# First norm's modulation columns: products on TensorE in four column groups in place of a chain on VectorE

## The reference

```python
mod = jax.nn.silu(c) @ w_ada[l] + b_ada[l]              # (1, 1024) @ (1024, 6144)
sh1, sc1, g1, sh2, sc2, g2 = jnp.split(mod, 6, axis=-1)
h = rms_norm(x, g_mix_norm[l]) * (1.0 + sc1[:, None]) + sh1[:, None]
proj = h @ w_in[l]                                      # q_lat (512 columns), kv_lat (256), ...
```

## Time and profile before

| | |
|---|---|
| device time, median of 3 runs | 1748.63 us (1746.57 to 1749.33) |
| span of the profiled execution | 1746.4 us |
| TensorE busy | 1692.4 us, 97% of the span |
| VectorE busy | 1093.3 us, 63% |
| ScalarE busy | 744.9 us, 43% |
| GpSimd busy | 298.0 us, 17% |
| mean granted TensorE clock | 0.992 |
| chain that ended last | TensorE 84%, VectorE 6%, ACT 4%, SP's queue 2% |

### The profile page before, as it was taken

The page is one execution under the profiler, slowest core; times in us unless marked ns, Lnnn a source line. Parts: engine busy times, 40 slices in busy tenths (PEclk is TensorE's granted clock), DMA queues, the critical chain, the costliest instruction groups (busy, mean ns, idle before and its releaser), DMA issues.

```text
span 1746.4 us, 32411 instructions
## 1 busy us (share of the span) xinstructions
PE 1692.4 (97%) x12781; PEld 1504.0 (86%) x12781; DVE 1093.3 (63%) x1748; ACT 744.9 (43%) x1111; POOL 298.0 (17%) x286
## 2 busy tenths in 40 slices
PE   5999999999999999899999999999999999999998
PEld 4776666788888888799999999999999999989986
DVE  6766576777764668855858664344753766754633
ACT  4467575454332342532323545346323643322323
POOL 2112196210000002432005221110102000000002
PEclk8999999999999999999999999999999999999999
DMA  9453532443333232264335752332543233332332
GB/s 310 124 141 102 157 110 84 135 97 107 99 95 98 84 108 67 85 172 124 127 105 152 224 141 87 99 117 80 166 117 96 74 94 91 92 97 85 96 95 75
DMA packets 321167, 201.18 MB, mean 115 GB/s; under 512 B 51279, under 2 KB 303814, under 8 KB 320918
## 3 DMA queue, kind: packets, MB, share of 16 engines
q1 hardware_dynamic: 300976, 160.79, 32.4%
q0 software_dynamic: 7952, 24.83, 4.7%
q10 hardware_dynamic: 12118, 13.88, 2.3%
HBM read 177.75 MB, written 17.24 MB: 112 GB/s over the span
## 4 chain that ended last, share of the span: by engine, by line
PE 84%; DVE 6%; ACT 4%; SPq 2%; issue 2%; DMA 1%; POOL 1%; ACTq 0%; DVEq 0%; POOLq 0%
PE ps L1467 69%; SPq L854 2%; PE ps L1608 1%; DVE wlo L2175 1%; PE ps L1769 1%; PE ps L1667 1%; PE ps L1779 1%; PE ps L1795 1%; PE ps L2020 1%; PE ps L1682 1%; PE ps L1584 1%; ACT whi L912 1%; DMA xrow<-in_x_dram 1%; PE ps L1946 0%; PE ps L1536 0%
## 5 line engine op out<-in xcount | busy, mean ns | idle before, releaser
L1467 PE MATMUL ps<-zhi,whi 128*128 128x258 f32 (+2 forms) x2072 | 639.2, 308 | 1.4 <-ACT ub L1201 0.6
L1467 PE MATMUL ps<-zlo,whi 128*128 128x258 f32 (+2 forms) x2072 | 633.4, 306 | 0.0
L1467 PE MATMUL ps<-zhi,wlo 128*128 128x258 f32 (+2 forms) x2072 | 632.1, 305 | 0.0
L1467 PEld LDWEIGHTS ps<-zhi,whi 128*128 128x128 f32 x2072 | 390.8, 189 | 25.5 <-issue 2.2
L2175 DVE TENSOR_TENSOR wlo<-stage,whi 128x1024 fp32r<-128x1024 f32 x256 | 324.9, 1270 | 136.0 <-ACT whi L912 124.0
L1467 PEld LDWEIGHTS ps<-zlo,whi 128*128 128x128 f32 x2072 | 390.2, 188 | 19.7 <-issue 1.2
L1467 PEld LDWEIGHTS ps<-zhi,wlo 128*128 128x128 f32 x2072 | 390.9, 189 | 18.0
L912 ACT ACTIVATE whi<-stage 128x1024 fp32r<-128x1024 f32 x256 | 269.4, 1055 | 305.2 <-PE ps L1467 253.7
L1467 PE MATMUL ps<-ghi,whi 128*128 128x512 f32 x340 | 134.7, 396 | 0.0
L1467 PE MATMUL ps<-glo,whi 128*128 128x512 f32 x340 | 134.2, 395 | 0.0
L1467 PE MATMUL ps<-ghi,wlo 128*128 128x512 f32 x340 | 134.0, 394 | 0.0
(11 more groups left out here) (432 smaller groups left out, 2833.5 us busy)
## 6 DMA issues: line engine op xcount, KB each, us to landing
stage<-in_w_up_dram SPq DMA_DIRECT2D x88, 512.0 KB, 3.8
stage<-in_w_in_dram SPq DMA_DIRECT2D x74, 512.0 KB, 4.0
stage<-in_w_down_dram SPq DMA_DIRECT2D x32, 512.0 KB, 4.0
ring<-in_w_ada_dram POOLq DMA_DIRECT2D x24, 512.0 KB, 4.4
adab<-in_w_ada_dram SPq DMA_DIRECT2D x16, 512.0 KB, 7.8
stage<-in_w_down_dram SPq DMA_DIRECT2D x16, 384.0 KB, 3.4
stage<-in_w_o_dram SPq DMA_DIRECT2D x8, 512.0 KB, 4.1
ring<-in_w_ada_dram SPq DMA_DIRECT2D x8, 512.0 KB, 3.7
```

The lines of the kernel that those rows point to most:

```text
L1467: last = pe.matmul(out, w(a, k), x(k, t0, t1), start=(k == 0 and a is whi and x is x_hi), stop=(k == ks - 1 and a is wlo))
```

## The change

The multiplication by silu(c) moves from VectorE to TensorE. `block_rows(r)` multiplies the blocks of round r, as moving columns, with weights `csil32` that hold column k of silu(c) 32 times. Four row tiles k go to the four groups of 32 PSUM partitions of bank 7 (m = 0 to 3), in two halves that add up: eight fp32 matmuls of 128x512 on 128*32 tiles. VectorE copies the bank to `acol`, and `block_sums` adds over the partitions with a column that is one on every 32nd partition.

Bank 7 is then no longer free for `scaled_turn`, which goes between banks 5 and 6 and waits for the zhi of the tile two before it. The transposes of most parameters and of the meta tokens (`setup_turns`) move behind turn 3, with their copies; only b_ada and g_mix are transposed first. SP's order is changed: two units of w_in go ahead of two w_ada blocks each. The order of TensorE's and VectorE's work is written anew.

```diff
+    misc[:, 2] = p % 32 == 0
...
-        XN_AT = (2, 3, 6, 7, 8, 9, 10, 11)
+        XN_AT = (3, 4, 5, 6, 9, 10, 11, 12)
+        MODULATED = (3, 6, 7, 8)
+        ROWS_MM, SUMS_MM = [2 * r + 1 for r in range(4)], [2 * r + 2 for r in range(4)]
+        NFIRST = ROW["g_ql"]
...
-            return ps[:, 5 + k % 3, :]
+            return ps[:, 5 + k % 2, :]
...
-            for u in range(4, 10):
+            for u in range(4, 8):
                 ada_block(u)
             load_unit(sp, 2, unit_views("ql", 2))
-            for u in range(10, 14):
+            for u in range(8, 12):
                 ada_block(u)
             load_unit(sp, 3, unit_views("ql", 3))
-            for u in range(14, 16):
+            for u in range(12, 16):
                 ada_block(u)
...
             act.activation(csil[:, :], ps[:, 2, 0:KD], ACT.Silu).then_inc(act_setup, 1)
+            act.activation(csil32[:, :, :], ps[:, 2, 0:KD].unsqueeze(2).to_broadcast([P, KD, 32]), ACT.Silu).then_inc(act_setup, 1)
...
             def scaled_turn(k):
 
-                if k == 2:
-                    pe.wait_ge(dve_setup, 3)
-                elif k > 2:
-                    pe.wait_ge(zhi_done, k - 2)
+                if k >= 2:
+                    pe.wait_ge(zhi_done, k - 1)
...
+            def block_rows(r):
+
+                if r:
+                    pe.wait_ge(acol_done, r)
+                else:
+                    pe.wait_ge(act_setup, 2)
+                for half in range(2):
+                    u = 4 * r + 2 * half
+                    for v in (u, u + 1):
+                        pe.wait_ge(bulk_in[v % 8], 16 * (v // 8 + 1))
+                    for m in range(4):
+                        mm = pe.matmul(ps[32 * m:32 * m + 32, 7, :].rearrange("p (a b) -> p a b", a=2),
+                                       csil32[:, 4 * half + m, :], adab[:, u:u + 2, m, :], start=half == 0, stop=half == 1)
+                mm.then_inc(mod_mm, 1)
...
+            block_rows(0)
+            pe.wait_ge(dve_setup, 1)
+            pe.wait_ge(xt_done, KD)
+            scaled_turn(0)
+            scaled_turn(1)
             block_sums(0)
             scaled_turn(2)
             first_products(0, (0, 1))
             first_products(1, (0, 1))
+            block_rows(1)
             scaled_turn(3)
+            setup_turns()
             block_sums(1)
-            scaled_turn(4)
+            pe.wait_ge(dve_setup, 5)
             first_products(0, (2,))
             first_products(1, (2,))
+            first_products(2, (0, 1, 2))
+            scaled_turn(4)
+            block_rows(2)
+            first_products(3, (0, 1, 2))
+            block_sums(2)
             scaled_turn(5)
-            block_sums(2)
-            first_products(2, (0, 1, 2))
-            first_products(3, (0, 1, 2))
-            scaled_turn(6)
-            scaled_turn(7)
             for k in range(4):
                 first_products(k, (3,))
+            first_products(4, range(4))
+            scaled_turn(6)
+            block_rows(3)
+            first_products(5, range(4))
             block_sums(3)
-            for k in range(4, KD):
-                first_products(k, (0, 1, 2))
-            for k in range(4, KD):
-                first_products(k, (3,))
+            scaled_turn(7)
+            first_products(6, range(4))
+            first_products(7, range(4))
...
+            def columns(r):
+
+                dve.wait_ge(mod_mm, ROWS_MM[r])
+                dve.tensor_copy(acol[r % 2][:, :, :], ps[:, 7, :].rearrange("p (a b) -> p a b", a=2)).then_inc(acol_done, 1)
...
+            columns(0)
+            split_lo(0)
+            modulation(0)
             split_lo(1)
-            modulation(0)
-            columns(1, 0, 2)
             z_low_first(0)
             z_low_first(1)
-            columns(1, 2, KD)
-            for r in (1, 2):
-                columns(r + 1, 0, 2)
-                modulation(r)
-                split_lo(r + 1)
-                columns(r + 1, 2, KD)
-                z_low_first(2 * r)
-                z_low_first(2 * r + 1)
+            columns(1)
+            setup_copies()
+            modulation(1)
+            split_lo(2)
+            z_low_first(2)
+            z_low_first(3)
+            columns(2)
+            modulation(2)
+            split_lo(3)
+            z_low_first(4)
+            z_low_first(5)
+            columns(3)
             modulation(3)
```

More of the change, by code:

```diff
@@ L621, in piece @@
             return t[0], len(t), 0 if GROUPS[g]["w"] == 64 else 2
-        n_par = sum(1 + ((ROW[n] + k - 1) // P - ROW[n] // P) for n, _, k in PARAMS) + 0
+        n_par = sum(1 + ((ROW[n] + k - 1) // P - ROW[n] // P) for n, _, k in PARAMS) - 2
         n_par2 = sum(r for _, _, r in HEAD_PARAMS)
@@ L1496, in scaled_turn, with setup_turns @@
             def scaled_turn(k):
-                if k == 2:
-                    pe.wait_ge(dve_setup, 3)
-                elif k > 2:
-                    pe.wait_ge(zhi_done, k - 2)
+                if k >= 2:
+                    pe.wait_ge(zhi_done, k - 1)
                 for t in range(QB):
-                    mm = pe.matmul(ps[:, 5 + k % 3, t * P:(t + 1) * P], xrow[:, t, k * P:(k + 1) * P], diag[:, t, :],
+                    mm = pe.matmul(ps[:, 5 + k % 2, t * P:(t + 1) * P], xrow[:, t, k * P:(k + 1) * P], diag[:, t, :],
                                    start=True, stop=True)
                 mm.then_inc(start_mm, 1)
[L1507 to L1521, removed]
+            def setup_turns():
+                pe.wait_ge(dve_setup, 2)
+                pe.wait_ge(s_par, 16 * n_par)
+                pe.wait_ge(s_par2, 16 * n_par2)
+                for b in range(NBLK):
+                    r = min(P, NROWS - b * P)
+                    mm = pe.transpose(ps[:, 1, b * P:b * P + r], prow[0:r, b, :], const("ident", r, r))
+                mm.then_inc(start_mm, 1)
+                pe.wait_ge(s_meta, 16)
+                for k in range(KD):
+                    mm = pe.transpose(ps[:, 3, k * META:(k + 1) * META], metar[:, k * P:(k + 1) * P],
+                                      const("ident", META, META))
+                mm.then_inc(start_mm, 1)
             def last_job(n, x_hi, x_lo, ks, between=None, behind=None):
@@ L2236, in table @@
                 dve.tensor_scalar(a, a, PI, -PI, ALU.min, ALU.max).then_inc(tab_ready, 1)
-            def column(r, k):
-                u = 4 * r + 2 * (k // 4)
-                o, w, c = acol[r % 2][:, :, :], adab[:, u:u + 2, k % 4, :], csil[:, k:k + 1]
-                if k % 4 == 0:
-                    for v in (u, u + 1):
-                        dve.wait_ge(bulk_in[v % 8], 16 * (v // 8 + 1))
-                if k == 0:
-                    if r >= 2:
-                        dve.wait_ge(mod_mm, r - 1)
-                    link(dve.tensor_scalar(o, w, c, None, ALU.mult))
-                elif k < KD - 1:
-                    link(dve.scalar_tensor_tensor(out=o, in0=w, scalar=c, in1=o, op0=ALU.mult, op1=ALU.add))
-                else:
-                    dve.scalar_tensor_tensor(out=o, in0=w, scalar=c, in1=o, op0=ALU.mult, op1=ALU.add).then_inc(acol_done, 1)
-            def columns(r, k0, k1):
-                for k in range(k0, k1):
-                    column(r, k)
+            def columns(r):
+                dve.wait_ge(mod_mm, ROWS_MM[r])
+                dve.tensor_copy(acol[r % 2][:, :, :], ps[:, 7, :].rearrange("p (a b) -> p a b", a=2)).then_inc(acol_done, 1)
             def modulation(r):
-                dve.wait_ge(mod_mm, r + 1)
+                dve.wait_ge(mod_mm, SUMS_MM[r])
                 for i in range(2):
```

39 lines of the change are left out of this document (21 added, 18 removed).

## The result

The changed kernel takes 1763.13 us (median of 6 runs, 1760.4 to 1765.85); the kernel before, timed beside it, 1748.01. The ratio is 1.0085, with a 95% interval from 1.0073 to 1.0096: it is slower, by 15.1 us, where 7.9 were forecast and 1762 was the top of the range. The profiled execution has a span of 1760.8 us, 14.4 more than before.

What follows compares the result with a forecast made beforehand. TensorE was taken to bound the kernel. Start -1.4, rows +5.55, setup turns +1.28, new waits +6.8, old waits -3.3, clock -1.0 make +7.9: span 1754.3, median 1756.5 us (2.2 above the span), range 1747 to 1762.

Steps and rivals of the forecast that it cites:

- What bounds the kernel, and the sign: Whole kernel: TensorE bounds it, VectorE's relief counts only where TensorE waited; slower 0.72, within 0.16, faster 0.12.
- The first product: Start of the first norm's products: 30.3 us instead of 31.66, a gain of 1.4.
- block_rows: Row blocks on TensorE: 1.85 us each, blocks 1 to 3 between products, +5.55; block 0 lies in the start.
- setup_turns: Parameter and meta-token transposes move from a wait at the start into the busy stretch: 0.62 + 0.66 = +1.28 us.
- Waits: First norm, TensorE: four new waits of 2.2, 1.2, 2.25 and 1.15 us, +6.8, against 3.3 that go.
- Rival 2: First norm: new waits close, first product before 29.3, later waits under 0.5 us in all; 1745.6 us, chance 0.12.
- Clock: First norm: denser work from 28.2 us puts fewer products into the first stretch at 1.2 GHz; -1.0 us.
- The second spell I keep: First norm: the second 1.2 GHz stretch, costing some 1.6 us, stays, since waits of 2.2 us like the one before it remain.
- A shift of 69.25 goes through to the end almost whole: Behind kvl's start at 69.25 us: later work only follows TensorE, so the shift to 77.2 reaches the end almost whole.
- 1 (the clock stays up): First norm: clock stays at 2.4 GHz, saving 1.05 on turn 2 and 1.5 and 1.6 after; 1752.3 us, chance 0.17.
- 3 and 4: Row blocks: column groups run in turn, 5.05 more each, 1774, chance 0.06; or overlap three quarters, 2.3 each, 1757.9, 0.06.
- The range: Whole kernel's median: 1747 to 1762 us, leaving out the closed-waits and column-groups-in-turn rivals, 0.18; the forecast's own was 1751.5 to 1761.

Runs made afterwards that it cites:

- rows_twice: The changed kernel with the row blocks of rounds 1 to 3 each computed twice on TensorE; 1763.06 us, 1.0088 of the kernel before.
- setup_back: The changed kernel with the setup turns moved into TensorE's wait before turn 2; 1762.64 us, 1.0084 of the kernel before.
- splits_early: The changed kernel with VectorE's splits of units 2 and 3 ahead of the copies of rounds 1 and 2; 1758.27 us, 1.0062 of the kernel before.
- tail_covered: The changed kernel with round 3's rows and sums earlier and job 3's products of tiles 4 to 7 last; 1754.77 us, 1.0042 of the kernel before.
- after_again: The changed kernel run once more, unedited, for a second trace; 1761.83 us, 1.0080 of the kernel before.
- late_11: The kernel before with 13 unused fp32 products of 512 columns put ahead of kvl, a shift of 11.2 us; 1758.30 us, 1.0066.
- after_bload: The changed kernel with GpSimd's loads, from braw on, issued four w_up jobs later; 1760.07 us, 1.0070 of the kernel before.
- filled: The changed kernel with four unused fp32 products of 512 columns in TensorE's wait before turn 2; 1763.49 us, 1.0084 of the kernel before.
- all_mended: The changed kernel with the edits of splits_early, tail_covered and setup_back together; 1751.09 us, 1.0021 of the kernel before.
- late_4: The kernel before with 5 unused fp32 products of 512 columns put ahead of kvl, a shift of 4.3 us; ratio 1.0034.

## Why the prediction was wrong, point by point

**What bounds the kernel, and the sign.** Held. TensorE was busy before, and relieving VectorE freed it mostly where nothing waited for it (by 18.6 us of busy time, where 21 were counted). The chain after is TensorE's from 28 us on but for the four new waits, where it runs through VectorE and ScalarE.

**The first product.** Forecast 30.3, measured 29.87; turn 2 took 2.08 at 1.2 GHz behind a wait of 3.68, forecast 3.8. The gain is 1.8 instead of 1.4.

**block_rows.** Forecast 1.85 a block and +5.55, measured 1.85 three times; rows_twice splits it into 1.72 and 0.13. The Trainium skill, page "TensorE: Matmul & The Clock Gate", section on measured speedup, has 3.07 for four row tiles, which gave the prediction's estimate of 2.2 to 2.4. Here eight matmuls take 1.72, against 6.9 for eight in a row at the 0.86 of the lat_stats matmul: a factor of 4.0, for fp32 and 512 columns, and the measurement decides. The Trainium skill, page "TensorEngine Tiling (Array Packing)", section on key properties, says that a change of tiling mode drains the engine. The 0.13 of a block is all that this could cost here.

**setup_turns.** Forecast 1.28, measured 0.99: the forecast added lengths of a timeline in which neighbours overlap, the chain doesn't. setup_back gets 1.0 back.

**Waits.** Forecast 2.2, 1.2, 2.25 and 1.15, 6.8 in all; measured 2.17, 1.17, 2.31 and 1.31, 6.96. Walking the queues in their written order, with durations of the kernel before, was good to 0.2 us each. splits_early and tail_covered confirm what each wait was for. Rival 2 (the waits close) is out.

**Clock: the first step that failed.** "The second spell I keep", -1.0. Low-clock busy time behind the first product was 5.6 + 3.4 = 9.0 us before; it is 3.5 + 5.4 + 2.9 = 11.9 after. At 0.43 for a product of 0.234, 46% of such time is loss: 4.1 before, 5.4 after, so the term is +1.3. The first spell was shorter, as forecast; the step left out that the wait of 2.17 us, behind turns and one-column sums at 38 to 40 us, came with a spell of 6.8 and not 3.4, and the wait of 2.31 before tile 6 with a third. splits_early and tail_covered show both to hang on these waits: each spell is gone with its wait. rows_twice shows that the wait is not enough, so no fixed price of one could have been read. The earlier trace rows had the pattern: both falls of the kernel before came after stretches in which TensorE mostly waited. With the measured terms the stage sums to -1.8 + 5.55 + 0.99 + 6.96 - 3.3 + 1.3 = +9.7. The 0.9 that are left of the 10.6 can be placed, to 0.1, by TensorE's timeline from start to start: the 96 products take 28.5 us instead of 26.6, so 0.5 more than the count above, the five turns 5.3 instead of 5.0, the sums 0.1 and the setup turns 0.1 more. In after_again the products take 29.3. So 2.7 of the miss are here, and the clock is by far the largest part of them, 2.3 or more.

**"A shift of 69.25 goes through to the end almost whole": held for the shift, failed as a total.** late_11 shows the shift itself at 10.95 for 11.2. But the step took for granted that the changed kernel adds nothing behind it, and 3.8 us of span came there: this is the second step that failed, a term put at nothing, and the larger one. 1.7 of them are the wait behind w_up's load, which after_bload removes. 0.4 come before the ada sums and 1.6 between TT and the end, at a spell of 1040.3 to 1043.7 and a wait on ko of 3.1 (1.4 before). Such places change from one execution to the next (after_again has a ko wait of 2.4 and no spell there, the second trace of the kernel before has neither), so this part isn't attributed. A spell near 725 to 742 us stands in nine of the ten traces with block_rows in every round except the profiled changed kernel's own, and in none of the other seven; its cause wasn't tried.

**Rivals.** 1 (the clock stays up): it fell three times. filled shows that the first spell goes if its wait is filled, for 1.5 to 2.1 us at kvl and nothing that can be measured at the end. 3 and 4: refuted by 1.85 and by rows_twice.

**The range** went to 1762 by "each of four waits off by half, either spell gone or doubled". It had no term for the 1670 us behind the stage, which the step above had declared empty. The median, 1763.13, lies 1.1 above its top, and that of after_again, 1761.83, just under it: near the edge the range was a matter of luck, but the centre, 1756.5, was 6.6 off, which are the 2.7 and the 3.8.

## What to carry to other kernels

Work taken off an engine that is busy 63% and put on one busy 97% stands in the chain at its full length: 5.55 us here. What it costs in the end depends on the waits and on the clock around it (5.2 us more cost 1.3 to 1.9 in rows_twice), but none of the orders tried made the changed kernel faster than the one before (all_mended, 1.0021). In a queue whose order is written by hand, put each split, copy and transpose ahead of long work that doesn't need it, and keep products in reserve for the last wait: three such moves took back 9.6 of 10.6 us at kvl. Price a new wait on TensorE with the clock spell it may bring, and give a shift of 10 us in a kernel of 1700 a term for what it meets later: here the one load that landed late.

## What the runs showed of the hardware that was not expected

- 5.2 us more of TensorE work in a stage with waits made it only 1.3 to 1.9 longer: with the same four waits there were 6.8 us at the low clock instead of 17.1.
- The same kernel has its spells in another order from one execution to the next: 6.8, 6.8 and 3.4 us, or 3.4, 6.8 and 6.8.
- Eight fp32 matmuls of 512 columns on 128*32 tiles run four side by side without loss: 1.72 us, where one such matmul on a 128*128 tile takes 0.86, plus 0.13 for entry and exit.
- A load of 512 KB that took 3.9 to 4.1 us with GpSimd's two loads of 256 KB moved away takes 5.5 or 9.5 beside them, with the same distances between the issues.
- A spell at half the clock can lie wholly in busy time: TensorE was busy 3.50 of 3.50 us from 904.1 in late_4. What went before it was a wait of 1.81 us that ended at 902.88. With 1.8 to 2.1 there (three traces) the spell came, with 1.0 to 1.3 (fourteen traces) it didn't.
- A spell near 725 to 742 us stands in nine of the ten traces that have block_rows in every round and with none of the other seven; its cause is open.
